# Residual held transposed in PSUM, samples' scatter behind the prompt's, embedding behind the fifteenth step, GpSimd summing the result's squares

## What is computed

```python
h = h + y @ w_out
h = h + moe(rmsnorm(h, g_ffn), w_r, b_r, w1, b1, w2, b2)   # 32 experts, 4 for each token
gate = sigmoid(rmsnorm(h, g_ple) @ w_pg + b_pg)
h = h + gate * (p @ w_pp)
return rmsnorm(h, g_final)

# moe, for each expert e, with the tokens' weights combine
hdn = xt @ w1[e] + b1[e]                                   # 1024 x 2048
gate = minimum(hdn[:, :1024], 7); up = clip(hdn[:, 1024:], -7, 7)
act = (up + 1) * gate * sigmoid(1.702 * gate)
out = out + combine[:, e:e + 1] * (act @ w2[e] + b2[e])    # 1024 x 1024
```

## Time and profile before

| | us |
|---|---|
| median of 3 runs | 1094.05 (1093.2 to 1094.35) |
| the profiled execution, its own time | 1091.18 |
| its span, first to last instruction | 1089.5 |
| PE busy | 1061.2 |
| VectorE busy | 385.1 |
| ScalarE busy | 168.2 |
| GpSimd busy | 13.8 |
| loaded from memory | 424.57 MB |

### The profile page before, as it was taken

How to read it: one execution, slowest core, us unless ns; L and a number is a source line. 1 busy time by engine, 2 the same in 40 slices (tenths; PEclk the granted TensorE clock), 3 DMA queues, 4 the chain that set the end, 5 groups by cost and what they waited for, 6 DMA issues and landing times.

```text
span 1089.5 us, 13468 instructions
## 1 busy us (share of the span) xinstructions
PE 1061.2 (97%) x5250; PEld 429.7 (39%) x5250; DVE 385.1 (35%) x875; ACT 168.2 (15%) x298; POOL 13.8 (1%) x20
## 2 busy tenths in 40 slices
PE   9999999999999999999999999999999999999996
PEld 7884433444333333333333333333333333333342
DVE  6563743222333333333333333333333332333326
ACT  2550600010000000000000000000000000000034
POOL 0100200000000000000000000000000000000000
PEclk9999999999999999999999999999999999999999
DMA  9957699998999999999999999999999999999941
GB/s 281 354 216 300 262 401 428 424 397 374 395 431 430 433 431 433 430 428 434 427 432 433 426 434 425 432 430 431 431 437 426 434 430 431 433 422 430 423 182 40
DMA packets 34312, 426.80 MB, mean 392 GB/s; under 512 B 5383, under 2 KB 8655, under 8 KB 16493
## 3 DMA queue, kind: packets, MB, share of 16 engines
q1 hardware_dynamic: 34284, 426.41, 93.6%
HBM read 424.57 MB, written 1.43 MB: 391 GB/s over the span
## 4 chain that ended last, share of the span: by engine, by line
PE 76%; DMA 22%; DVE 1%; ACT 0%; SPq 0%; issue 0%; DVEq 0%
PE bank L1669 29%; DMA ring<-in_w 21%; PE bank L1710 17%; PE bank L1344 5%; PE bank L1599 5%; PE bank L1581 3%; PE bank L1432 3%; PE bank L1607 2%; PE bank L1592 2%; PE bank L1689 2%; PE bank L1767 1%; PE bank L1779 1%; DMA w_in<-in_w_in 1%; PE bank L1695 1%; PE bank L1654 1%; PE bank L1534 1%
## 5 line engine op out<-in xcount | busy, mean ns | idle before, releaser
L1669 PE MATMUL bank<-ring,xgT 128*64 128x512 f32 x2048 | 447.5, 593 | 14.5 <-DMA ring<-in_w 14.5
L1669 PEld LDWEIGHTS bank<-ring,xgT 128*64 128x64 f32 x2048 | 145.5, 137 | 298.3 <-issue 267.6
L1710 PE MATMUL bank<-ring,actT 128*64 128x512 f32 x1024 | 233.6, 598 | 0.0
L1177 DVE TENSOR_SCALAR gmin<-bank 128x512 f32<-128x512 f32 x32 | 22.1, 692 | 338.9 <-PE bank L1669 338.9
L1710 PEld LDWEIGHTS bank<-ring,actT 128*64 128x64 f32 x1024 | 67.9, 136 | 141.4 <-issue 120.5
L700 ACT ACTIVATE sig<-gmin 128x512 f32<-128x512 f32 x32 | 20.1, 630 | 446.4 <-DVE gmin L1177 446.4
L1131 DVE TENSOR_TENSOR h<-bank,h 128x512 f32<-128x512 f32 x132 | 84.8, 684 | 8.7 <-PE bank L1599 7.6
L1085 DVE TENSOR_TENSOR xgT<-bank,vecT 128x512 f32<-128x512 f32 x32 | 22.1, 692 | 155.9 <-PE bank L1592 155.2
L1171 DVE TENSOR_SCALAR wpick<-slot_no,pos,share 128x128 f32<-128x128 f32 (+1 forms) x96 | 27.1, 339 | 112.5 <-PE bank L1669 112.5
L1599 PE MATMUL bank<-y,wpickT 64*128 64x512 f32 x264 | 65.6, 615 | 0.8 <-ACT y L711 0.8
L711 ACT ACTIVATE y<-bank 128x512 f32<-128x512 f32 x32 | 19.1, 597 | 237.5 <-PE bank L1710 237.5
(11 more groups left out here) (306 smaller groups left out, 645.6 us busy)
## 6 DMA issues: line engine op xcount, KB each, us to landing
ring<-in_w SPq DMA_DIRECT2D x53, 4096.0 KB, 32.0
ring<-in_w SPq DMA_DIRECT2D x86, 2048.0 KB, 28.4
w_in<-in_w_in SPq DMA_DIRECT2D x3, 2048.0 KB, 14.2
w_out<-in_w_out SPq DMA_DIRECT2D x1, 4096.0 KB, 17.0
w_pg<-in_w_pg SPq DMA_DIRECT2D x4, 1024.0 KB, 26.7
h<-in_x_prompt SPq DMA_DIRECT2D x2, 512.0 KB, 3.9
w_in<-in_w_in SPq DMA_DIRECT2D x2, 512.0 KB, 7.8
w_in<-in_w_in SPq DMA_DIRECT2D x1, 1024.0 KB, 10.8
```

What stands on the lines that cost most here:

```text
L1669: ins = pe.matmul(bank[part][r, :], xgT[:, (k % FOUR) * W1_QUADS + k // FOUR, :], w[:, c:c + HALF], start=False, stop=(k == W1_SLOTS - 1), ...
L1710: ins = pe.matmul(bank[2][CAP * m:CAP * (m + 1), :], actT[:, half:half + CAP], pair[:, c:c + HALF], start=(f == 0), stop=(f == FF // P - 1 ...
```

## The change

- The residual h is brought into PSUM once, in step 0, transposed: `residual(b)`, block b of 128 channels x 256 prompt tokens, two blocks to a bank, banks 4 to 7 (`residual_in`). It stays there to the end. The scatter now loads y (64 rows x 128 channels) and streams `wpickT` (256 columns), accumulating onto it; nothing is added by VectorE.
- The 8 samples are kept transposed in SBUF (`hT_samples`). Their scatter stands right behind the prompt's: eight products of 8 columns, into a free corner of banks 0 and 2, which VectorE adds in two small additions.
- The embedding moves behind the fifteenth step and is made transposed, tokens as columns (`pwT`).
- At the end nothing of h is turned. The gate is made transposed, eight blocks of 128 channels x 264 tokens; norm, sigmoid, embedding and residual go block by block. The squares of the first norm are reduced by VectorE and spread by one product; those of the last by GpSimd (six additions) and six passes of PE. Each block, times g_final, is turned back by PE and scaled by the root as it leaves PSUM.
- b_pg and g_final come as columns with the other vectors at the start (two more small loads); the two spread loads go.
- The last y is copied out in halves.

```diff
@@ the scatter
-            def scatter(t, rows, first_bank):
-                for m in range(2):
-                    r = slice(CAP * m, CAP * (m + 1))
-                    ins = pe.matmul(bank[first_bank + m][0:rows, :], wpickT[r, t * P:t * P + rows], y[r, :],
-                                    start=True, stop=True)
-                ins.then_inc(spread, 1)
-            def scatter_samples(first_bank):
-                for m in range(2):
-                    r = slice(CAP * m, CAP * (m + 1))
-                    ins = pe.matmul(bank[first_bank][32 * m:32 * m + NS, :], wpickT[r, SEQ:T], y[r, :],
-                                    start=True, stop=True)
-                ins.then_inc(spread, 1)
+            def residual_in():
+                for b in range(KD):
+                    for t in range(2):
+                        pe.matmul(residual(b)[:, t * P:(t + 1) * P], h[:, t, b * P:(b + 1) * P], ident[:],
+                                  start=(b % 2 == 0 and t == 0), stop=False, skip_group_check=True)
+            def scatter(blocks=range(KD // 2), last=False):
+                for c in blocks:
+                    for m in range(2):
+                        r, b = slice(CAP * m, CAP * (m + 1)), KD // 2 * m + c
+                        ins = pe.matmul(residual(b), y[r, c * P:(c + 1) * P], wpickT[r, 0:SEQ], start=False, stop=last,
+                                        skip_group_check=True)
...
+            def samples_in():
+                pe.wait_ge(steps_ready, 1)
+                for b in range(KD):
+                    c = SAMPLES_AT + b * NS
+                    ins = pe.transpose(bank[2][:, c:c + NS], h[0:NS, 2, b * P:(b + 1) * P], ident[0:NS, 0:NS])
+                ins.then_inc(turned, 1)
+                pe.wait_ge(h_added, NT + 1)
+            def scatter_samples(blocks=range(KD // 2)):
+                for c in blocks:
+                    for m in range(2):
+                        r = slice(CAP * m, CAP * (m + 1))
+                        at_c = (0 if m else T) + c * NS
+                        ins = pe.matmul(bank[2 * m][:, at_c:at_c + NS], y[r, c * P:(c + 1) * P], wpickT[r, SEQ:T],
+                                        start=True, stop=True, skip_group_check=True)
...
@@ a step of PE
                 pe.wait_ge(y_ready, i + 1)
-                pe.wait_ge(h_added, i * 2 * NT + NT)
-                scatter(0, P, 4)
-                scatter(1, P, 6)
+                if started:
+                    samples_in()
+                    residual_in()
+                scatter()
+                pe.wait_ge(gmin_ready, i + 1)
+                scatter_samples()
...
                 ins.then_inc(wpick_turned, 1)
-                scatter_samples(4)
-
                 pe.wait_ge(actT_ready, i + 1)
@@ the end of GpSimd's program
+            pool.wait_ge(last_squared, 2)
+            link(pool.tensor_tensor(token_sums[:, 1, :], squares[:, 0, :], squares[:, 1, :], ALU.add))
+            for b in range(2, KD - 1):
+                pool.wait_ge(last_squared, b + 1)
+                link(pool.tensor_tensor(token_sums[:, 1, :], token_sums[:, 1, :], squares[:, b, :], ALU.add))
@@ the end on VectorE
+            dve.tensor_reduce(token_sums[:, 0, :], squares[:].rearrange("p b t -> p t b"), AX.X, ALU.add
+                              ).then_inc(sums_ready, 1)
...
+            def normal(b):
+                dve.wait_ge(plegate_made, b + 1)
+                dve.tensor_tensor(gate[:, b, :], bank[GATE_BANKS[b]][:, 0:T], rstd_wide[:], ALU.mult
+                                  ).then_inc(plebias_ready, 1)
+            def add_embedded(b):
+                dve.wait_ge(plegate_ready, b + 1)
+                link(dve.tensor_tensor(gate[:, b, :], gate[:, b, :], pwT[:, b, :], ALU.mult))
+                dve.tensor_tensor(gate[:, b, SEQ:T], gate[:, b, SEQ:T], hT_samples[:, b, :], ALU.add)
+                dve.tensor_tensor(gate[:, b, 0:SEQ], gate[:, b, 0:SEQ], residual(b), ALU.add).then_inc(h_final, 1)
@@ the end on PE
+                for j, k in enumerate((0, 4, 1, 5, 2, 6, 3, 7)):
+                    if b == 0:
+                        pe.wait_ge(wpg_in[k // 2], 16)
+                        wait_tail(k)
+                    ins = pe.matmul(bank[GATE_BANKS[b]][:, 0:T], w_pg[:, k, b * P:(b + 1) * P], tail_nT[:, k, :],
+                                    start=(j == 0), stop=(j == KD - 1), skip_group_check=True)
```

More of the change, by code:

```diff
@@ new lines, in square_and_scale @@
+            def square_and_scale(b):
+                act.wait_ge(h_final, b + 1)
+                act.activation(scaled[:, b, :], gate[:, b, :], ACT.Identity, scale=vcol("g_final", b)
+                               ).then_inc(scaled_act, 1)
+                act.activation(squares[:, b, :], gate[:, b, :], ACT.Square).then_inc(last_squared, 1)
+            for b in range(KD - 1):
+                sigmoid_of(b)
+                if b > 0:
+                    square_and_scale(b - 1)
+            square_and_scale(KD - 2)
@@ new lines, in _ @@
+            add_embedded(KD - 2)
+            normal(KD - 1)
+            add_embedded(KD - 1)
+            dve.wait_ge(h_final, KD)
+            dve.tensor_tensor(squares[:, KD - 1, :], gate[:, KD - 1, :], gate[:, KD - 1, :], ALU.mult
+                              ).then_inc(sums_ready, 1)
+            dve.tensor_scalar(scaled[:, KD - 1, :], gate[:, KD - 1, :], vcol("g_final", KD - 1), None, ALU.mult
+                              ).then_inc(scaled_dve, 1)
+            dve.wait_ge(rms_ready, 6)
@@ new lines, in scatter @@
+            def scatter(blocks=range(KD // 2), last=False):
[4 more added lines that the diff above has]
+                                        skip_group_check=True)
+                        if last and c % 2:
+                            ins.then_inc(spread, 1)
+                if not last:
+                    ins.then_inc(spread, 1)
@@ L1728, in _ @@
             n = blocks * PERIOD + LAST
-            with pe.Fori(1, blocks) as period:
+            with pe.Fori(1, EMBED_BLOCK) as period:
+                for r in range(PERIOD):
+                    step(period, r)
+            pe.wait_ge(wpickT_ready, EMBED_BLOCK * PERIOD + 1)
+            pe.wait_ge(h_added, EMBED_BLOCK * PERIOD + NT + 1)
+            pe.wait_ge(wpp_in, 32)
+            for b in range(KD):
+                embed(b)
+            pe.wait_ge(pw_ready, KD)
+            with pe.Fori(EMBED_BLOCK, blocks) as period:
                 for r in range(PERIOD):
@@ new lines, in last_sums @@
+            def last_sums(src, first):
+                for t, rows in TILES:
+                    ins = pe.matmul(bank[1][0:rows, t:t + 1], src[:, t * P:t * P + rows], group_sum[:, 0:1], start=first and t == 0,
+                                    stop=not first, skip_group_check=True)
+                return ins
+            pe.wait_ge(tail_nT_dve, 1)
+            for b in range(KD):
+                if GATE_BEFORE[b] is not None:
+                    pe.wait_ge(plebias_ready, GATE_BEFORE[b] + 1)
+                for j, k in enumerate((0, 4, 1, 5, 2, 6, 3, 7)):
[4 more added lines that the diff above has]
+                                    start=(j == 0), stop=(j == KD - 1), skip_group_check=True)
+                ins.then_inc(plegate_made, 1)
+                if b == 1:
+                    spread_sums()
+                if b == 4:
+                    pe.wait_ge(rms_ready, 5)
+                    pe.wait_ge(h_final, 2)
+                    turn_back(0)
+                    turn_back(1)
+                if b == 5:
+                    turn_back(2)
+                if b == 6:
+                    pe.wait_ge(h_final, 4)
+                    pe.wait_ge(plebias_ready, 3)
+                    for q in (3, 4):
+                        turn_back(q)
@@ new lines, in _ @@
+            turn_back(5)
+            turn_back(6)
+            pe.wait_ge(h_final, 6)
+            for b in range(4):
+                turn_back_samples(b)
+            pe.wait_ge(plebias_ready, KD)
+            for b in range(4, KD - 1):
+                turn_back_samples(b)
+            pe.wait_ge(pool_done, POOL_SUMS)
+            last_sums(token_sums[:, 1, :], True)
+            pe.wait_ge(sums_ready, 2)
+            last_sums(squares[:, KD - 1, :], False).then_inc(last_sums_made, 1)
+            turn_back(KD - 1)
```

407 lines of the change are left out of this document (163 added, 244 removed).

## The result

The changed kernel took 1086.09 us in the median (1085.31 to 1088.0), the kernel before, on the same chip, 1093.62 (1093.11 to 1094.35): a ratio of 0.9933, 95% interval 0.9916 to 0.995. Forecast was 1088.0 in a range of 1085 to 1096. The profiled execution took 1086.36, its span 1084.6. So the time is right; not each of its terms is.

A forecast was written before the change was run, and what follows sets the result against it. Memory, not PE, was taken to set the loop's pace. Loop -1.9 and end -4.2 make -6.1 on the profiled 1091.18, so 1085.1; plus 2.9 to the median gives 1088.0 us, range 1085 to 1096.

The forecast's parts named there:

- One step: Each expert-loop step: W2 starts 0.53 us earlier, the samples' products add 0.83, the scatter 0.01; +0.3 us.
- Step 0: First step of the expert loop: turning the samples and bringing the residual into PSUM cost PE 5.1 us.
- the hole: New gap in the memory loads at about 158 to 163 us, because W2's slots free late: some 5.4 us.
- the holes saved: Load gaps the old embedding caused between 222 and 309.5 us, 7.8 in all, vanish but for some 0.5.
- The embedding: Moved from steps 2 and 3 to behind the fifteenth step: 7.9 us of PE, absorbed by waits for data.
- the cover: PE's 17 us of waiting for data in the loop, said to absorb the embedding; without it, 7.9 us.
- The loop's end: Memory still decides by 4.7 us: step 31 starts at 1014.6, and the last W2 ends 1.9 us earlier.
- The end: From the last W2 to the span's end: 3.4 + 30.4 + 9.7 = 43.5 us for 47.7, so -4.2.
- Profile to median: The old median's 2.9 us above its profiled execution carries over, taking 1085.1 to 1088.0 us.
- A: Samples' loads in the loop don't pair, PE becomes the bound, a step grows 1.24 us: 1114 us; chance 0.18.
- B: PE idles between gate blocks, so the closing part gives nothing back: 1092.2 us; chance 0.14.
- C: Memory's load holes only move, the first step's costing what the embedding's gave: 1089.9 us; chance 0.08.

The follow-up runs named there:

- run 1: The changed kernel run again without any edit, for a second trace: 1085.93 us, ratio 0.9932 to the kernel before.
- run 12: Changed kernel with the embedding moved between the last two steps and the loop made one again: 1093.38 us.
- run 5: The kernel before, run again without any edit for a second trace: 1092.81 us.
- run 11: Changed kernel with the six additions of the result's squares moved from GpSimd to VectorE: 1086.31 us, ratio 0.9942 to the kernel before.
- run 7: Changed kernel with PE's loop behind the embedding split into two loops, so its code is one block longer, same work: 1089.66 us.
- Run 8: Changed kernel with the embedding moved behind step 4, ahead of the loop, and the loop made one again: 1088.27 us.
- run 6: Changed kernel with the residual's 16 products replacing four idle products that PE issues while waiting for the router: 1085.98 us.
- run 9: Changed kernel with the residual in the idle products' place, plus four filler products of 8 columns ahead of the loop: 1083.29 us.
- run 10: Changed kernel with four of its seven first warm-up products left out, moving PE's later code by 16 instructions: 1092.05 us.
- run 2: Changed kernel with the residual added behind the fifteenth step, the first scatter of each bank beginning the sum: 1085.08 us.

## Why the prediction came true, point by point

- **One step**: +0.3 forecast, +0.26 measured (27.83). By the chain of waits the samples take 0.79 for 0.83, as pairs, and the scatter 1.93, as before (1.92); the forecast's 1.73 and 1.72 leave the same 0.2 out on both sides. From the start of the gather to that of W2 it is 3.07 us for 3.65, 0.58 less where 0.53 was forecast. From the trace's step (start, length, engine; in brackets idle before), behind it the gather of the step in the earlier trace rows:

```profile
401.74 2.00 PE L1578 MATMUL bank<-wpickT,y 64*128 64x256 f32 x16
403.57 0.96 PE L1600 MATMUL bank<-wpickT,y 64*128 64x8 f32 x16
404.45 1.49 PE L1552 MATMUL bank<-x_parts,pick 128*64 128x512 bf16 x12
...
407.52 2.80 PE L1701 MATMUL bank<-ring,actT 128*64 128x512 f32 x12 [0.31 <-ACT actT L720]
```

```profile
380.21 1.49 PE L1581 MATMUL bank<-x_parts,pick 128*64 128x512 bf16 x12
```

- **Step 0** +4.8 for 5.1, the hole 4.3 for 5.4, the holes saved 6.9 for 7.3. That would be 2.6 us of data ahead for 1.9; 0.3 were lost ahead of the hole and 0.4 between 320 and 740 us, where eleven code packets come, so 1.95 were left. The mechanism is right; that the sum fits to 0.05 is luck (run 1 has 2.54).
- **The embedding**: 8.3 for 7.9, and absorbed; run 12 shows that without the cover it costs 7.4.
- **The loop's end: wrong.** "Memory lets it: 1014.6" took the loads' mean for the load. In the first trace step 31 started at 1016.29, because of the 1.95 us nothing reached the slowest engine. What was in order there: +0.57 for two and a half steps, and step 31 itself 1.0 shorter (26.09 from its start to the copy of y before, 25.07 now; 0.8 forecast). So y was copied 0.45 us earlier and not 1.9. In run 1 step 31 did start at 1014.5, but PE then waited in it, and y was copied at 1040.52, 1.3 us earlier than in the earlier trace rows. Short in both, by 1.45 and 0.6.
- **The end**: -4.5 for -4.2, each of its three parts within 0.2, and the same in both traces (43.26 from the copy of y). Inside, several prices were off. The reduction read across blocks took 3.96 for 2.35. PE asked for the sums at 1051.84, they were there at 1051.57; so PE just didn't wait. GpSimd's additions took 0.74 to 0.81 for 0.55 and were done at 1074.87, 1.0 us early. The five stores issued 0.47 apart for 0.66, and from the last to the span's end it was 3.1 us for 2.0, which nearly cancel. The part up to the gate names four terms that make 3.1 of its 3.4.
- **Profile to median: wrong.** 2.9 us were carried over. The changed kernel's profiled execution lies 0.3 above its median, and run 5 shows why the old one lay so far below: the clock held in its embedding. The change's embedding, passes of 264 columns, had a granted clock of 1.00 in all traces. So of the 7.5 us some 4.5 are the end, and some 1.6 the old embedding's clock if a median execution of before is like run 5 (that most are is inferred from the times and the mean clocks in run 5, not seen in traces); the rest is the loop. From the start of step 0 to the copy of y it is 909.3 and 910.9 us in the two traces of before, 908.7 and 908.5 in those of the changed kernel: 0.7 to 0.8 us less than the quick execution, 2.2 to 2.4 less than the other. Two errors, 1.45 short in the loop and 3.2 over in the carry, went against each other; that the forecast lies 1.9 us from the measured time is luck.
- **Rivals.** A's mechanism is real and its price was wrong: unpaired, a step is 0.73 longer than before, and the kernel is as slow as before (1.0011, 1.0002 to 1.002). That is the point that the forecast named, "from +0.7 the kernel is slower"; 1114 was not. B did not come: no idle PE between gate blocks. C came in another guise, and in part: the holes are fewer, but what they gave was lost again, all of it in the first trace and a third in run 1.
- **The skill's two rules.** The trace agrees with the Trainium skill, "TensorEngine Tiling (Array Packing)", section "Tiling Modes": loads of upper and lower rows overlap (0.049 us each, 0.079 in a row of their own). Sixteen loads at full price, 1.7 us, were not seen in either order. The shared port remains untried: in the end GpSimd's additions and VectorE's hardly ran at one time, and run 11 shows no difference. Nor do the two additions of the earlier trace rows show it: the slower one writes bf16 and the faster fp32, and GpSimd was at work in 0.64 of its 1.73 us.

What is open: that code packets drive the engines apart is shown by the 43 growths of the spread, each with a packet, and by run 7, which adds packets and no work. Run 8 changes the holes along with the packets, and in runs 6, 9 and 10 the time follows PE's stop and not the spread. Which engine a packet hits, and why eight of the 16 are spared, was not seen. Nor why a loop is fetched again at one place in the code and not 16 instructions further.

## What to carry to other kernels

Where memory decides, count what the slowest of the DMA engines delivers, not the mean rate: a gain in bytes is only a gain if the last of the 16 landings moves. Before a change of a loop's surroundings is judged, look whether the code packets (q8) and waits on "issue" changed, since they can be worth as much as the edit; in run 10, 16 instructions fewer ahead of the loop cost 12.3 us in two of its steps. And read more than one execution before a profile's distance to the median is carried over.

## What had not been expected of the hardware

- A 16 KB packet of code took 0.9 to 1.1 us in nearly all cases. The spread of the loads' landings grew with single packets by up to 1.6 us, and where no packet followed it stayed (4.5 us from 694 to 930 in the changed kernel). It fell where the memory gave less than its 431 GB/s: 2.1 to 1.3 us at the hole of 158 to 164 us (changed kernel), 4.4 to 3.0 in run 10 between 611 and 621, where the memory gave 391 to 418 GB/s. At the load of 967 us, 14 packets behind the last hole had left a spread of 3.5 to 5.6 us (runs 1 and 9 at the ends, 4.6 in the changed kernel's first trace), 23 one of 6.0 and 7.1 (runs 6, 2), 29 one of 6.5 (run 7).
- A loop of five steps may run its second round without a packet of code (changed kernel, runs 9 and 11), or be fetched again, with PE standing for 3.2 to 9.2 us (runs 2, 6, 7, 10). The Trainium skill, "Runtime: NRT & Kernel Launch", section "Instruction fetch mechanics", says that code comes in blocks of 16 KiB and that a taken branch to a block outside the current window of two stalls until it is fetched. The stops agree; the rounds without a packet do not, since a round of this loop brings some six packets when it is fetched (300 to 409 us in the changed kernel) and its branch back goes further than two blocks. The section calls the cost of crossing a block mostly hidden; the landings here show a cost that falls on the data.
- VectorE's reciprocal of 128 x 264 fp32 took 1.80 us, where a multiplication of the size takes 0.43.
